# Seven-product gate and up in an FFN kernel: the high and low part of n in one 512-column matmul, ScalarE seeding PSUM banks, VectorE adding the halves

## What is computed

```python
x = x + 0.5 * swiglu(rms_norm(x, ffn1_norm[l]), ffn1_gate[l], ffn1_up[l], ffn1_down[l])
...
f = (jax.nn.silu(h @ w_gate[l]) * (h @ w_up[l])) @ w_down[l]
```

## Time and profile before

| | us |
|---|---|
| median of 3 runs (1793.57 to 1793.69) | 1793.64 |
| the profiled execution, first to last instruction (its span; the profile gives no other time of its own) | 1791.9 |
| three stretches of seven-product groups, together | 399 |
| TensorE busy | 1784.2 |
| DVE busy | 1368.7 |
| ACT busy | 958.7 |

### The profile page before, as it was taken

One profiled execution on the slowest core, in us unless ns is written; L12 is line 12 of the kernel. 1 busy time (PEld: TensorE's weight loads), 2 busy tenths in 40 slices (PEclk: granted clock), 3 DMA queues, 4 the chain that ended last, 5 costly groups with the idle time before them and its releaser, 6 DMA issues.

```text
span 1791.9 us, 28282 instructions
## 1 busy us (share of the span) xinstructions
PE 1784.2 (100%) x11580; PEld 1589.9 (89%) x11580; DVE 1368.7 (76%) x1696; ACT 958.7 (54%) x1422; POOL 147.5 (8%) x127
## 2 busy tenths in 40 slices
PE   9999999999999999999999999999999999999998
PEld 8899999988779888889998998878888898999887
DVE  5888799956686555588878997655777579887898
ACT  6455467565444444445544755445776464554584
POOL 0000000225430200200000003100000000000000
PEclk9999999999999999999999999999999999999999
DMA  6233443532215232323334344433332323334444
GB/s 189 71 112 101 118 159 124 165 106 95 72 48 165 71 113 91 103 72 96 113 100 159 124 148 138 141 106 106 106 94 95 95 72 89 103 113 121 137 144 154
DMA packets 229165, 202.83 MB, mean 113 GB/s; under 512 B 9814, under 2 KB 194219, under 8 KB 229035
## 3 DMA queue, kind: packets, MB, share of 16 engines
q1 hardware_dynamic: 228192, 200.44, 36.2%
q0 software_dynamic: 144, 0.52, 0.2%
q10 hardware_dynamic: 698, 0.05, 0.0%
HBM read 189.97 MB, written 2.62 MB: 107 GB/s over the span
## 4 chain that ended last, share of the span: by engine, by line
PE 99%; DVE 0%; DVEq 0%; ACT 0%; POOL 0%; issue 0%; POOLq 0%
PE bank L750 16%; PE bank L752 16%; PE bank L751 16%; PE bank L971 7%; PE bank L972 7%; PE bank L969 7%; PE bank L882 4%; PE bank L883 4%; PE bank L884 4%; PE bank L874 2%; PE bank L872 2%; PE bank L873 2%; PE bank L812 2%; PE bank L813 2%; PE bank L814 2%; PE bank L1418 1%
## 5 line engine op out<-in xcount | busy, mean ns | idle before, releaser
L750 PE MATMUL bank<-n_hi,w_hi 128*128 128x512 f32 (+1 forms) x1160 | 453.6, 391 | 0.0
L752 PE MATMUL bank<-n_hi,w_lo 128*128 128x512 f32 (+1 forms) x1160 | 445.6, 384 | 0.0
L751 PE MATMUL bank<-n_lo,w_hi 128*128 128x512 f32 (+1 forms) x1160 | 445.3, 384 | 0.0
L2355 DVE TENSOR_TENSOR w_lo<-w_raw,w_hi 128x2048 fp32r<-128x2048 f32 x88 | 201.5, 2290 | 156.8 <-ACT w_hi L1553 156.6
L971 PE MATMUL bank<-n_sums_lo,w_hi 128*128 128x256 f32 x1092 | 309.2, 283 | 0.0
L972 PE MATMUL bank<-n_sums_hi,w_lo 128*128 128x256 f32 x1092 | 309.1, 283 | 0.0
L969 PE MATMUL bank<-n_sums_hi,w_hi 128*128 128x256 f32 x1092 | 309.1, 283 | 0.0
L752 PEld LDWEIGHTS bank<-n_hi,w_lo 128*128 128x128 f32 x1160 | 218.0, 188 | 43.7
L750 PEld LDWEIGHTS bank<-n_hi,w_hi 128*128 128x128 f32 x1160 | 218.2, 188 | 41.9 <-issue 1.7
L751 PEld LDWEIGHTS bank<-n_lo,w_hi 128*128 128x128 f32 x1160 | 218.4, 188 | 40.6 <-issue 1.0
L1553 ACT CAST w_hi<-w_raw 128x2048 fp32r<-128x2048 f32 x88 | 167.8, 1907 | 157.3 <-PE bank L752 140.5
(11 more groups left out here) (451 smaller groups left out, 3482.9 us busy)
## 6 DMA issues: line engine op xcount, KB each, us to landing
w_raw<-in_w_in SPq DMA_DIRECT2D x68, 512.0 KB, 4.6
w_raw<-in_ffn_down SPq DMA_DIRECT2D x36, 512.0 KB, 4.1
w_raw<-in_ffn_up SPq DMA_DIRECT2D x54, 256.0 KB, 3.8
w_raw<-in_ffn_gate SPq DMA_DIRECT2D x53, 256.0 KB, 3.0
w_raw<-in_w_down SPq DMA_DIRECT2D x18, 512.0 KB, 4.3
w_raw<-in_ffn_gate SPq DMA_DIRECT2D x17, 512.0 KB, 4.0
w_raw<-in_ffn_up SPq DMA_DIRECT2D x17, 512.0 KB, 5.3
w_raw_extra<-in_ffn_down SPq DMA_DIRECT2D x16, 512.0 KB, 3.8
```

Of the source, the lines that this page charges most:

```text
L750: pe.matmul(acc, w_hi, x_hi, start=start, stop=False)
L751: pe.matmul(acc, w_hi, x_lo, start=False, stop=False)
L752: return pe.matmul(acc, w_lo, x_hi, start=False, stop=stop)
L2355: dve.tensor_tensor(wlo[par][:, :], raw[par][:, :], whi[par][:, :].bitcast(F32), ALU.subtract).then_inc(w_lo_ready, 1)
```

## The change

- `n_high` and `n_low` parts of n lie side by side in one tensor, `nhl`. A product's first two matmuls (high weight by high n, high weight by low n) become one matmul of 512 columns, whose moving operand is a run of 256 high and a run of 256 low values, written to the two halves of the bank. The low weight by high n still adds 256 columns to the first half. The wanted sum is now the sum of the two halves of a bank.
- Y (S1) and the first A11 of an FFN keep the old three matmuls (`short_product`).
- ACT no longer copies X to SBUF at the first two points: it copies the whole bank to Z's and V's bank (`bank[X + 1]`, `bank[X + 3]`), and TensorE adds A12 and S4 onto it. At the third point X goes to `tmp` and `sumsq`, and V likewise (`read_v`).
- In TensorE's queue A22 moves ahead of A12, and V's S4 behind X's S3. A dummy matmul in the first group writes V's bank once.
- The halves are added on DVE: `fold_x`, `fold_z`, and a 512-wide add of `tmp` and `sumsq` in `add_y`; `add_v` goes, `add_z` stays for the first group only, as two adds. Before each fold ACT copies the low half to SBUF (`read_low_half`). The second silu runs on SBUF like the first.

```diff
...
+FOLDS = 3 * SEVEN + 1
 SUMS_AT, HALVES_AT = down_from(SUMS, 3 * SEVEN), down_from(HALVES, SEVEN + 1)
 RING_HI_AT, RING_LO_AT = down_from(RING_HIGHS, 4), down_from(RINGS, 4)
-DONE_AT, ADDED_AT = down_from(DONE, 2 * SEVEN), down_from(ADDED, 2 * SEVEN)
+DONE_AT, ADDED_AT = down_from(DONE, 3 * SEVEN), down_from(ADDED, FOLDS)
 S_AT, H_HI_AT, H_AT = down_from(4 * HC, 12), down_from(HC, 3), down_from(HC, 1)
 LOADED_AT = [down_from(192, 64 * sum(c % 2 == n for c in range(HEAD, TAIL))) for n in range(3)]
-READS = 3 * SEVEN
+READS = 6 * SEVEN - 1
 def silu_count(f, j):
...
         ypost = at("y_post", [P, C, T], F32, n_at)
         sq_at = cursor[0]
         sq = [sb(f"sq{s}", [P, T], F32) for s in range(2)]
-        tmp = [sb(f"tmp{s}", [P, T], F32) for s in range(2)]
+        sumsq_at = cursor[0] + 4096
+        parts = sb("tmp_sumsq", [P, 3, T], F32)
+        tmp = [parts[:, s] for s in range(2)]
+        sumsq = parts[:, 2]
+        ups = parts[:, :, :].rearrange("p n (s t) -> p n s t", s=2)
...
-        sumsq_at = cursor[0]
-        sumsq = sb("sum_squares", [P, T], F32)
...
-        nh = at("n_sums_hi", [P, 7, C // 2, T // 2], F32R, arena + 44 * KB)
-        nl = at("n_sums_lo", [P, 7, C // 2, T // 2], F32R, arena + 72 * KB)
+        nhl = at("n_sums_hi_lo", [P, 2, 7, C // 2, T // 2], F32R, arena + 44 * KB)
+        nh, nl = nhl[:, 0], nhl[:, 1]
         nf = at("n_sums", [P, 7, C // 2, T // 2], F32, arena + 72 * KB)
...
             def seven_products(f, base):
-                reads, h0, sums0 = READS * f, FC * f, RING_LO_AT[f] - 4
+                reads, h0, sums0, folds = READS * f, FC * f, RING_LO_AT[f] - 4, ADDED_AT[f] - FOLDS
+
+                def both(b):
+
+                    return bank[b][:, :].rearrange("p (s t) -> p s t", s=2)
                 def product(acc, par, pos, slot, begin):
+
+                    for kk in range(C // 2):
+                        w0 = T * pos + P * kk
+                        pe.matmul(both(acc), whi[par][:, w0:w0 + P], nhl[:, :, slot, kk, :], start=begin and kk == 0, stop=False,
+                                  skip_group_check=True)
+                        mm = pe.matmul(bank[acc][:, HALF[0]], wlo[par][:, w0:w0 + P], nh[:, slot, kk, :], start=False,
+                                       stop=kk == C // 2 - 1, skip_group_check=True)
+                    return mm
+
+                def short_product(acc, par, pos, slot):
                     for kk in range(C // 2):
                         out_, w0 = bank[acc][:, HALF[0]], slice(T * pos + P * kk, T * pos + P * kk + P)
-                        pe.matmul(out_, whi[par][:, w0], nh[:, slot, kk, :], start=begin and kk == 0, stop=False,
-                                  skip_group_check=True)
+                        pe.matmul(out_, whi[par][:, w0], nh[:, slot, kk, :], start=kk == 0, stop=False, skip_group_check=True)
                         pe.matmul(out_, whi[par][:, w0], nl[:, slot, kk, :], start=False, stop=False, skip_group_check=True)
                         mm = pe.matmul(out_, wlo[par][:, w0], nh[:, slot, kk, :], start=False, stop=kk == C // 2 - 1,
                                        skip_group_check=True)
...
                     elif i == 1:
                         pe.wait_ge(gu_scaled, 2 * (h0 + HEAD))
                     else:
-                        pe.wait_ge(silu_ready, silu_count(f, c - 1))
-                    product(X, 0, 1, A11, True).then_inc(c_done, 1)
-                    if i > 1:
-                        pe.wait_ge(gu_scaled, 2 * (h0 + c - 1))
-                    mm = product(Z, 0, 0, A12, True)
+                        pe.wait_ge(c_steps, folds + 3 * (i - 2) + 4)
+                    (product(X, 0, 1, A11, True) if i else short_product(X, 0, 1, A11)).then_inc(c_done, 1)
                     if i:
-                        pe.wait_ge(p_copied, reads + 3 * i)
-                        mm = product(before, 0, 2, A22, False)
-                    mm.then_inc(unit_done, 1)
+                        pe.wait_ge(p_copied, reads + 6 * i - 3)
+                        product(before, 0, 2, A22, False)
+                        pe.wait_ge(p_copied, reads + 6 * i - 1)
+                    product(Z, 0, 0, A12, i == 0).then_inc(unit_done, 1)
                     pe.wait_ge(w_lo_ready, first + 2)
                     if i == 0:
                         pe.wait_ge(ring_lo, sums0 + 3)
-                    pe.wait_ge(p_copied, reads + 3 * i + 1)
+                        pe.wait_ge(p_copied, reads + 1)
+                        pe.matmul(both(V), whi[1][:, 0:P], nhl[:, :, S2, 0, :], start=True, stop=True)
                     product(X, 1, 0, S2, False).then_inc(c_done, 1)
-                    product(Y, 1, 1, S1, True).then_inc(w_half, 1)
-                    product(V, 1, 3, S4, True)
+                    if i > 1:
+                        pe.wait_ge(gu_scaled, 2 * (h0 + c - 1))
+                    short_product(Y, 1, 1, S1).then_inc(w_half, 1)
                     if i == 0:
                         pe.wait_ge(ring_lo, sums0 + 4)
-                    pe.wait_ge(p_copied, reads + 3 * i + 2)
-                    product(X, 1, 2, S3, False).then_inc(unit_done, 1)
+                    pe.wait_ge(p_copied, reads + 6 * i + 2)
+                    product(X, 1, 2, S3, False).then_inc(c_done, 1)
+                    product(V, 1, 3, S4, False).then_inc(unit_done, 1)
                 def last_product():
                     pe.wait_ge(w_lo_ready, seven_unit(base, TAIL, 0) + 1)
-                    pe.wait_ge(p_copied, reads + READS)
+                    pe.wait_ge(p_copied, reads + READS - 2)
                     product(4 if (TAIL - 1) % 2 == 0 else 0, 0, 0, A22, False).then_inc(unit_done, 1)
                 return last_product
...
             def seven_steps(f, base):
                 s0, sums0, halves0 = S_AT[f] - 12, SUMS_AT[f] - 3 * SEVEN, HALVES_AT[f] - SEVEN - 1
-                done0, added0 = DONE_AT[f] - 2 * SEVEN, ADDED_AT[f] - 2 * SEVEN
+                done0, added0 = DONE_AT[f] - 3 * SEVEN, ADDED_AT[f] - FOLDS
                 def n_high(slots, steps):
...
                     op = act.copy(whi[1][:, 0:2 * T], wide[c % 2][:, T:3 * T])
                     if i < 2:
                         op.then_inc(h_hi_ready, 1)
+                    if i:
+                        read_x(c - 1, 3)
                     act.wait_ge(unit_done, first)
                     act.copy(whi[1][:, 2 * T:4 * T], wide[c % 2][:, 3 * T:5 * T]).then_inc(w_hi_ready, 1)
+                def up_parts(c, half):
+
+                    return ups[:, c % 2::2 - c % 2, half, :]
+
                 def read_x(c, n):
                     i, X = c - HEAD, 0 if c % 2 else 4
-                    if n == 1:
-                        act.wait_ge(h_product, FC * f + c - 1)
-                    act.wait_ge(*((unit_done, seven_unit(base, c, 1) + 1) if n == 3 else (c_done, done0 + 2 * i + n)))
-                    dst = sq[c % 2][:, HALF[0]] if n == 1 else tmp[c % 2][:, HALF[n - 2]]
-                    act.copy(dst, bank[X][:, HALF[0]]).then_inc(p_copied, 1)
-
...
+                    act.wait_ge(c_done, done0 + 3 * i + n)
+                    if n == 3:
+                        act.wait_ge(gu_scaled, 2 * (FC * f + c))
+                        op = act.copy(up_parts(c, 1), bank[X][:, :].rearrange("p (s t) -> p s t", s=2))
+                    elif n == 2 or i:
+                        op = act.copy(bank[X + (1 if n == 1 else 3)][:, :], bank[X][:, :])
+                    else:
+                        op = act.copy(sq[c % 2][:, HALF[0]], bank[X][:, HALF[0]])
+                    op.then_inc(p_copied, 1)
+
+                def read_v(c):
+
+                    act.wait_ge(unit_done, seven_unit(base, c, 1) + 1)
+                    act.copy(up_parts(c, 0), bank[3 if c % 2 else 7][:, :].rearrange("p (s t) -> p s t", s=2)).then_inc(p_copied, 1)
+
+                def read_low_half(c, half):
+
+                    b = (0 if c % 2 else 4) + (0 if half else 1)
+                    act.wait_ge(unit_done, seven_unit(base, c + half, 0) + 1)
+                    act.wait_ge(h_product, FC * f + c - 1)
+                    act.copy(sq[c % 2][:, HALF[half]], bank[b][:, HALF[1]]).then_inc(p_copied, 1)
+
+                def silu_half(c, half):
+
+                    act.wait_ge(c_steps, added0 + 3 * (c - HEAD) + (4 if half else 2))
+                    part = sq[c % 2][:, HALF[half]]
+                    act.activation(part, part, ACT.Silu).then_inc(silu_ready, 1)
                 for j in range(3):
                     if j:
...
                 silu(f, 4)
                 n_high(slice(S3, S3 + 1), 9)
                 high_b(HEAD)
+                act.wait_ge(h_product, FC * f + HEAD - 1)
                 read_x(HEAD, 1)
                 for c in range(HEAD + 1, TAIL):
+                    if c > HEAD + 1:
+                        read_low_half(c - 2, 1)
+                        read_low_half(c - 1, 0)
                     high_a(c)
                     if c == HEAD + 1:
```

(64 more changed lines are left out.)

8 lines of the change are left out of this document (removed).

## The result

The changed kernel takes 1818.54 us (1817.94 to 1818.62, four runs) against 1793.66 for the kernel before, a ratio of 1.0137 with a 95% interval of 1.0124 to 1.0149. The forecast was 1813.1 in a range of 1800 to 1826: slower as forecast, by 24.9 us instead of 19.5.

What follows compares the result with a forecast made beforehand. The prediction took a DVE-ACT loop of 10.50 us a group, above the old 10.08, as the bound; with first-group delays this cost 6.5 us a stretch, 19.5 for three, so 1793.6 + 19.5 = 1813.1 us, range 1800 to 1826.

Steps and rivals of the forecast that it cites:

- TensorE waits before S3, released by ACT's copy of a bank.: Sign in the new trace: TensorE idle some 0.7 us per group before the first matmul of S3.
- the last pause of 0.6: End of a stretch: one last TensorE pause, 0.6 us, counted into the 6.5 us a stretch.
- The matmuls: TensorE's fused products: 1.387 us instead of 1.44, saving 0.053 each, 11.6 us for three FFNs.
- The TensorE-ACT loop: From T (start of a group's second unit) through ACT's reads, split, silus, copy, then five products: 10.45 us a group.
- The bank-to-bank copy: ACT's 512-wide copy of X between banks: taken as 0.59 us, between 0.37 and 1.05.
- rival 3: ACT's bank-to-bank copy is the bound: at 0.9 us, 10.76 a group, some 1822 us; chance 0.10.
- The DVE-ACT loop: DVE's splits, sums, adds and folds with ACT's casts and `read_x(c-1, 3)`: 10.50 us a group.
- The loop does not contain TensorE at all. So I take 10.50: DVE-ACT loop taken to set the group at 10.50 us, with TensorE waiting 0.7 per group before S3.
- The first group: Start of each stretch: TensorE waits 1.0 and 0.5 us once, making T of group 7 1.4 late.
- The sum: Loss of 6.5 us a stretch, 19.5 for three, giving 1813.1 us.
- What follows has slack: After each stretch: the next unit's splits end some 0.7 us before they are wanted.
- Rival 1: TensorE still binds and the pauses vanish: 9.77 us a group, 11.6 saved, 1782.0 us; chance 0.07.

Runs made afterwards that it cites:

- run 6: Changed kernel with ACT's copy for V between the two casts of `high_a` and `read_x(c-1, 3)` ahead of `high_b`: 1796.91 us, 1.0016 of the kernel before.
- run 7: Changed kernel with ACT's reads, copies and silus and DVE's `fold_z` and `sumsq` add reordered, same operations: 1792.23 us, 0.9990 of the kernel before.
- run 8: The reordered kernel of run 7 with each fused pair as two matmuls of 256 columns again: 1798.18 us, 1.0024 of the kernel before.
- run 2: Changed kernel with the 512-wide add of `sumsq` in `add_y` cut to one column: 1815.85 us, 1.0123 of the kernel before.

## Why the prediction was right, and which terms were off

- **The cause** was as put: ACT and DVE no longer fit beside TensorE, because steps were added to chains that come round once a group. Runs 6 and 7 show it, where order alone brings back 22 and 26 us.
- **"TensorE waits before S3, released by ACT's copy of a bank."** 33 of the 36 waits for line 1739, which together are 17.9 us on the matmul's own row and 25.8 counted from the weight load. Right in place; per group 0.50 or 0.7, as one counts. Groups 7 to 17 have it; the last pause of 0.6 that I reckoned with, in group 18, did not come.
- **The matmuls**, 0.053 a fused product: mis-sized. I took 0.2267 from the row nearest in width. Mostly it was 0.233, 7 ns below the upper bound of 0.240, so a product saves 0.027, and runs 7 and 8 differ by 0.026 a product. Some runs of pairs did come at the sum that I took, 0.3467. The Trainium skill (TensorE: Matmul & The Clock Gate, "Back-to-back issue gap") puts about 2.5 ns on top of the columns of an isolated matmul, which would be what a pair saves; by the rows of before it would be 13.3. Mostly measured were 6.7, so this trace agrees with neither.
- **The TensorE-ACT loop**, 10.45: mis-sized, 10.65 in run 2. The products are 0.13 of the 0.20, the silus 0.12, and 0.05 goes the other way, from T to ACT's start.
- **The bank-to-bank copy**, taken as 0.59 between 0.37 and 1.05: 0.58 to 0.59 (line 1739), the same as from a bank to SBUF (0.58, line 1737). So rival 3 is gone. The Trainium skill (ScalarE: Activation LUTs, the note on ScalarE to PSUM in "Step-by-step: what each stage is for") has ScalarE write faster to PSUM than to SBUF; this trace shows no such gain.
- **The DVE-ACT loop**, 10.50: by its own steps 10.54 now. One term was off: after the new 512-wide add the next starts 0.79 later, not 0.72 (114.01 to 114.80).
- **"The loop does not contain TensorE at all. So I take 10.50"**: the step that failed. Two loops were longer, and TensorE is in both. One is the TensorE-ACT loop with its true terms, 10.65. The other I had not seen. In my own numbers ACT was ready for its second cast at T + 6.50 and TensorE's unit ended, as ACT sees it, at T + 3.51 + 2.77 + 0.25 = T + 6.53. A tie, which I read as slack. The loop that runs through this tie, the copy, S3, V, second cast, `low_b`, adds, folds, silu, has by the trace 0.63 (copy and listed restart, 105.82 to 106.45) + 2.93 (S3 and V, to 109.38) + 0.20 + 1.08 + 2.21 + 1.14 + 0.79 + 0.60 + 0.33 + 0.77 = 10.68, which is the measured group. The tie alone adds little: without it the group would still be 10.65, as run 2 has it.
- **The first group**, 1.0 and 0.5: measured 0.98 and 0.56 from the weight load.
- **The sum.** The time was missed by 5.4 us (24.9 against 19.5). The stretches grew by 7.9, 8.1 and 7.8 us where I had 6.5 each (the first, from its first matmul to the one behind it, from 133.09 to 140.97). In that one, eleven groups came 2.0 us later than reckoned, and the last pause, 0.6, stayed away. Over the three stretches it makes 4.3 of the 5.4, and the waits behind the stretches, in the next point, are 1.1.
- **"What follows has slack"**: nearly. Behind two stretches TensorE waits 0.5 us, 1.1 together, for the split of unit 21, which DVE does after its large sums.
- **Rival 1**, TensorE still the bound, is what run 7 makes of the same instructions: its price of -11.6 us was too high, since it rested on 0.053; run 7 is 1.7 below the kernel before by the medians, with its waits at the ends still in. The change alone does not reach it.

## What to carry to other kernels

Where several engines hand work round in a ring, write down every closed loop of waits and sum it: the longest sets the period, shortening another brings nothing, and an engine that is 77% busy can lie on the loop that holds the ring. Put a copy that another engine waits for ahead of work that nobody waits for yet, and look whether the place lies on a further loop. A tie between two arrivals is not slack: it joins two loops, and the joint one can be longer than both. Loops within 0.2 us of each other, as here, change places when terms are off by that much, so sum and test those next to the longest too.
